# Recurrent mixer, output projection and layer norm of three tiles placed beside the third attention, and modulation chunks spaced out

## The chip, the cores and the metric

The kernel runs on one core of a Trainium2 chip, as one program written engine by engine: TensorE (PE) multiplies, VectorE (DVE), ScalarE (ACT) and GpSimd (POOL) do the elementwise work, SyncE (SP) issues the weight transfers. The metric is the device time of one execution in microseconds. All data are float32. A float32 matmul shows in the trace as two weight loads and two matmul instructions.

## What is computed

Three transformer-like layers over 512 tokens (4 tiles of 128) of width 1024:

```python
# layers 0 and 1: adaptive modulation, two attentions each
mod = silu(c) @ w_ada[layer] + b_ada[layer]          # 1024 x 3072, per layer: shift, scale, gate
h = rmsnorm(x, g_pre) * (1 + scale) + shift
y = even_mixer(h) if layer == 0 else odd_mixer(h)    # (mla + window) or (differential + forgetting)
x = x + gate * rmsnorm(y, g_post)
# layer 2
h = x @ w_in
o_nsa = compressed, selected and window attention, 6 heads
o_sb  = stick_breaking(...)                          # 4 heads
o_hg  = hgrn2_mixer(...)                             # 6 heads, a recurrence over the tokens:
#   b = cumsum(log f);  att[t, s] = sum_d q[t,d] k[s,d] exp(b[t,d] - b[s,d])
#   o = att @ v + (q * exp(b)) @ state;  state = exp(b_last) * state + (k * exp(b_last - b)).T @ v
o_hg = o_hg * rsqrt(mean(o_hg^2) + eps) * hg_norm_w
mixed = concat(o_nsa, o_sb, o_hg) * silu(z)
out = layer_norm(ALPHA * x + mixed @ w_out)
```

## The kernel before

**Attention as a sequence of steps.** `attention(L)` (L = 0, 1, 2) walks over value units, one per head and tile of 128 queries: 64, 48 and 88 of them. In step r TensorE issues the scores of the unit two ahead (`LOOK`, L879), waits for the probabilities of this unit and transposes them (L894), and multiplies the previous unit with its values (L857). DVE masks and takes the row maximum (L1952), ACT takes the exponential (L1320) and copies the transposed block (L1168). Each engine runs its own instructions strictly in the order written, so a wait in one holds everything behind it. Scores and transposes have two buffers each, probabilities four.

**Fill.** Between these, `filler(n)` gives TensorE other matmuls, one contraction step of a 128x512 tile at a time: projections not needed yet, or output projections of finished tiles. `FILLERS[L]` lists weight chunks with their tiles in order, `SPREAD[L]` says (number of tiles, over how many steps), `UNITS` how many fill units a tile has (8 if not listed). `tile_done` on DVE and ACT evicts a tile in the step in which it ends; slower sequences (`chains`) advance by one stage a step.

**Weights.** `ring` has three slots of 2 MB. Chunk n goes to slot n mod 3, and SP waits until the chunk three before it has been used (L709).

**First attention.** Its fill is seven gate tiles (steps 0 to 19), then the eight chunks of `w_ada` for the gate of layer 0 and the modulation of layer 1 (steps 20 to 33): `adas` sums a chunk with 32-column matmuls (L811), `adac` or `adag` (L796, L803) add its strips. Then tiles 0 to 2 of the output projection and the input transposes of layer 1. In front of chunk (0, 5) SP also issues the replication `rel_rows` (L699), in front of (1, 4) two rows (L702, L703).

**Third attention.** Groups: for each query tile the heads of the compressed, selected and window branches, then at the end the stick-breaking heads of all four tiles (steps 72 to 87). Its fill is seven weight chunks, over 82 of the 88 steps. `hf` starts the forget-gate chain `forget_tile`, three times, with a reciprocal on DVE (L1848). POOL forms the recurrence's operands: `differences(c)` (15 instructions), then ACT's `exponentials(c)` (L1351 to L1356), then `operands(c)` (16 instructions), all from L1540; chunks 0 and 1 of these are started in the last steps (`HG_EARLY`).

**Recurrence, after the attention.** For each tile c: level products of three pairs of heads, written into the score and transpose banks (L1087, L1090), their sums on DVE (L1632), `outputs` (L1103, L1108), the state update (L1135), the head norm; beside it the output tile of c-1: transposes `mT` (L910), two `y` halves (L920), layer norm over DVE and ACT, two passes on POOL (L1540) and the store. Tile 3 comes last.

## Time and profile before

| | us |
|---|---|
| median of three runs | 1452.41 |
| lowest, highest | 1451.28, 1458.86 |
| the profiled execution | 1457.49 |
| its span, first to last instruction | 1455.7 |
| TensorE busy | 1280.3 (88%) |
| VectorE busy | 553.7 (38%) |
| ScalarE busy | 427.3 (29%) |
| GpSimd busy | 112.3 (8%) |
| mean granted TensorE clock | 0.911 |

Numbers of TensorE instructions are larger than those of matmuls in the code, since each float32 matmul is two. The granted clock is relative to 2.4 GHz; 0.5 is the lower of the two levels, 1.2 GHz.

### The profile page before, as it was taken

To read this page: it belongs to the slowest core of one execution; us is meant where nothing else is said; L and a number is where in the kernel's file an instruction comes from. 1 tells how busy PE (TensorE), PEld (TensorE's weight loads), DVE (VectorE), ACT (ScalarE), POOL (GpSimd) and SP (SyncE) were. 2 spreads that over 40 slices of the span, in tenths; PEclk is the share of its full clock that TensorE was granted. 3 is DMA by queue.
4 is the path that set the end of the run, shared out by engine and by line. 5 is a ranking of instruction groups with operands and counts; after the bars stand their busy time and mean duration, and the time that the engine had idled before them with its cause. 6 is when DMAs were issued, how large, how long until landed. Compare 5 with 4: busy or idle time off the path is not lost.

```text
span 1455.7 us, 15110 instructions
## 1 busy us (share of the span) xinstructions
PE 1280.3 (88%) x5264; PEld 706.9 (49%) x5264; DVE 553.7 (38%) x1422; ACT 427.3 (29%) x1086; POOL 112.3 (8%) x140
## 2 busy tenths in 40 slices
PE   4989989679998999989999989989998999966974
PEld 1555555335554444334455555555453555545541
DVE  3233223323445420234442433112124731667871
ACT  0133025313433101322224322114233543651211
POOL 0000000000001000000000000000000000384722
PEclk7889999868988999999999999989998999956987
DMA  9221311468000430242111005241101111000000
GB/s 349 80 87 48 126 58 58 159 218 227 1 1 1 116 58 16 61 100 58 58 59 58 1 1 139 59 159 44 44 0 44 44 59 58 1 0 31 1 30 29
DMA packets 60258, 99.71 MB, mean 69 GB/s; under 512 B 12068, under 2 KB 22129, under 8 KB 60184
## 3 DMA queue, kind: packets, MB, share of 16 engines
q1 hardware_dynamic: 54370, 93.58, 20.7%
q10 hardware_dynamic: 5814, 5.18, 1.1%
q8 instruction: 43, 0.70, 0.2%
q14 instruction: 31, 0.25, 0.1%
HBM read 96.60 MB, written 4.08 MB: 69 GB/s over the span
## 4 chain that ended last, share of the span: by engine, by line
PE 72%; DVE 13%; ACT 5%; DMA 4%; issue 3%; POOL 2%; ACTq 1%; SPq 0%; DVEq 0%; POOLq 0%
PE PR L827 29%; PE SC L879 7%; PE OB L857 6%; PE PT L739 6%; PE PR L739 4%; PE OB L739 4%; PE SC L739 4%; DMA ring<-in_w_ada 4%; PE PT L894 3%; PE PR L920 3%; DVE d L1632 2%; DVE stage L1632 2%; POOL arena L1540 2%; PE PR L811 1%; DVE tok L1632 1%
## 5 line engine op out<-in xcount | busy, mean ns | idle before, releaser
L827 PE MATMUL PR<-ring,hT 128*128 128x512 f32 (+1 forms) x784 | 380.2, 599 | 6.9 <-DVE hT L1671 4.1
L1320 ACT ACTIVATE stage<-stage,nmax 128x256 f32<-128x256 f32 (+7 forms) x200 | 103.7, 519 | 350.3 <-DVE nmax L1952 328.1
L827 PEld LDWEIGHTS PR<-ring,hT 128*128 128x128 f32 x784 | 137.0, 198 | 115.9 <-issue 96.4
L857 PEld LDWEIGHTS OB<-arena,pts 128*128 128x128 f32 (+3 forms) x880 | 133.7, 205 | 104.8 <-issue 84.0
L879 PE MATMUL SC<-arena 64*128 64x256 f32 (+15 forms) x432 | 150.5, 459 | 10.0 <-DVE nmax L1952 10.0
L827 PE MATMUL PR<-hT,ring 128*128 128x512 f32 (+1 forms) x304 | 155.1, 634 | 0.0
L1540 POOL TENSOR_TENSOR arena<-arena 128x192 f32<-128x192 f32 (+1 forms) x118 | 80.1, 679 | 830.7 <-PE OB L857 782.8
L857 PE MATMUL OB<-arena,pts 128*128 128x64 f32 (+4 forms) x880 | 134.2, 283 | 9.9 <-ACT pts L1168 9.9
L894 PEld LDWEIGHTS PT<-ident,stage 128*128 128x128 f32 (+3 forms) x440 | 58.4, 147 | 124.3 <-issue 59.0
L894 PE MATMUL PT<-ident,stage 128*128 128x128 f32 (+3 forms) x440 | 87.7, 291 | 29.8 <-ACT stage L1299 12.2
L1168 ACT ACTIVATE pts<-PT 128x256 f32<-128x256 f32 (+7 forms) x200 | 80.7, 404 | 52.7 <-issue 19.7
L1952 DVE CUSTOM_DVE_ANT_0 stage<-SC,causal 128x128 f32<-128x128 f32 (+3 forms) x96 | 47.2, 491 | 115.7 <-issue 52.9
L827 PEld LDWEIGHTS PR<-hT,ring 128*128 128x128 f32 (+1 forms) x304 | 52.3, 194 | 57.2 <-issue 55.9
L879 PEld LDWEIGHTS SC<-arena 64*128 64x128 f32 (+2 forms) x432 | 62.7, 194 | 25.0 <-DVE nmax L1952 10.4
L1952 DVE CUSTOM_DVE_ANT_0 stage<-SC,arena 128x128 f32<-128x128 f32 (+7 forms) x72 | 28.0, 388 | 119.8 <-PE SC L879 59.5
L920 PE MATMUL PR<-ring,hT 128*128 128x512 f32 x128 | 63.3, 649 | 6.1 <-DVE hT L2176 6.1
L739 PE MATMUL PR<-ring,hT 128*128 128x512 f32 (+5 forms) x160 | 51.8, 481 | 3.9 <-ACT hT L1211 2.0
L739 PE MATMUL SC<-ring,hT 128*128 128x512 f32 (+3 forms) x144 | 51.2, 515 | 0.0
L739 PE MATMUL PT<-ring,hT 128*128 128x512 f32 (+4 forms) x144 | 50.0, 502 | 0.0
L920 PEld LDWEIGHTS PR<-ring,hT 128*128 128x128 f32 x128 | 25.8, 209 | 36.1 <-issue 29.5
L1636 DVE TENSOR_SCALAR t<-PR 128x512 f32<-128x512 f32 (+3 forms) x29 | 17.4, 600 | 64.9 <-PE PR L827 53.7
L739 PEld LDWEIGHTS PR<-ring,hT 128*128 128x128 f32 x160 | 28.6, 203 | 24.0 <-issue 17.7
(337 smaller groups left out, 1300.2 us busy)
## 6 DMA issues: line engine op xcount, KB each, us to landing
ring<-in_w_ada SPq DMA_DIRECT2D x12, 2048.0 KB, 18.6
ring<-in_od_w_in SPq DMA_DIRECT2D x8, 2048.0 KB, 14.2
ring<-in_w_in SPq DMA_DIRECT2D x5, 1536.0 KB, 6.7
ring<-in_ev_w_in SPq DMA_DIRECT2D x3, 2048.0 KB, 7.9
ring<-in_w_in SPq DMA_DIRECT2D x3, 2048.0 KB, 9.7
ring<-in_ev_w_out SPq DMA_DIRECT2D x2, 2048.0 KB, 8.0
ring<-in_od_w_out SPq DMA_DIRECT2D x2, 2048.0 KB, 8.6
ring<-in_w_out SPq DMA_DIRECT2D x2, 2048.0 KB, 7.8
```

Source lines behind the costliest of these rows:

```text
L739: mm = pe.matmul(dst, lhs(k), rhs(k), start=(k == 0), stop=(k == K - 1))
L827: mm = pe.matmul(dst, l, r, start=(k == 0), stop=(k == KT - 1))
L857: mm = pe.matmul(ob[:, h * w:h * w + w], pts[0:rows_, v % 2, n * P:n * P + P], vb, start=(n == 0), stop=(n == len(blocks) - 1))
L879: pe.matmul(SC[s % 2][:, 0:n], q, k, start=True, stop=True).then_inc(s_done, 1)
L894: tr = pe.transpose(PT[v % 2][0:w, b * P:b * P + P], pb[:, s % NP, b * P:b * P + w], ident[:, :])
L920: mm = pe.matmul(b[:, :], hT[:, k, i * P:i * P + P], W[:, k, :], start=(k == 0), stop=(k == KT - 1))
L1168: return act.activation(dst, src, ACT.Copy, scale=scale)
L1320: give(act.activation(pb[:, s % NP, 0:n], zm[:, s % 2, 0:n], ACT.Exp, bias=nmax[:, row, c:c + 1], scale=-1.0, accum_out=rsum[:, row, c:c + ...
L1540: return pool.tensor_tensor(dst, a, b, op)
L1632: return dve.tensor_tensor(dst, a, b, op)
L1636: return dve.tensor_scalar(dst, a, s1, None, op0)
L1952: give(dve.tensor_tensor_reduce(out=z, in0=SC[s % 2][:, 0:n], in1=mask, scale=-scale, scalar=start, op0=ALU.add, op1=ALU.min, accum_out=nm ...
```

## The change

Three things, besides what they need in buffers.

1. In the first attention each `w_ada` chunk is followed by a gate tile, over four steps a pair. The two gate chunks keep their ring slots for that long and all eight `w_ada` chunks use the remaining slot (`ring_slots`). A chunk's strip sum comes after the next chunk's matmuls.
2. In the third attention the stick-breaking heads move to steps 18 to 33, behind tile 0 of the other branches. The projections are done by step 37. Steps 38 to 87 are filled with the recurrence of all four tiles and the output projection and layer norm of tiles 0 to 2. The level products become one tile per head (24 instead of 12 pairs), in the two banks of the fill, with their sums on DVE (`level_sums`) per head as well; head norm and layer norm become chains over steps. `exponentials(c)` starts at steps 26, 38, 49 and 60 and takes three steps. POOL makes differences and operands as early as the buffers allow, and its four output tiles last. The ring slot of `nz` and parts of `hT`, `grow`, `window` hold what stood in the score banks and the arena; two ring slots are left for the weights of that phase.
3. Small moves: in attention 1 `next_input(2, 0)` comes before tile 2's output; `finish_gates()` comes first among DVE's evictions of a step.

Behind the attention only tile 3 remains: `mT`, `y`, layer norm, store.

```diff
+def strip_sum(chunk_):
+
+    return ("adag", chunk_[0], chunk_[1] - 4) if chunk_[1] >= 4 else ("adac", *chunk_)
+
+
+STRIP_CHUNKS = [(0, 4), (1, 0), (0, 5), (1, 1), (1, 2), (1, 4), (1, 3), (1, 5)]
+GATES = [("gate0", 1, 0), ("gate0", 0, 1), ("gate0", 1, 1), ("gate0", 0, 2), ("gate0", 1, 2), ("gate0", 0, 3),
+         ("gate0", 1, 3)]
...
 FILLERS = [
-    [(("w", "gate0", 0), [("gate0", 0, i) for i in range(1, T)]),
-     (("w", "gate0", 1), [("gate0", 1, i) for i in range(T)])]
-    + [(("ada", 0, 4), [("adas", 0, 4)]), (("ada", 1, 0), [("adas", 1, 0), ("adag", 0, 0)]),
-       (("ada", 0, 5), [("adas", 0, 5), ("adac", 1, 0)]), (("ada", 1, 1), [("adas", 1, 1), ("adag", 0, 1)]),
-       (("ada", 1, 2), [("adas", 1, 2), ("adac", 1, 1)]), (("ada", 1, 4), [("adas", 1, 4), ("adac", 1, 2)]),
-       (("ada", 1, 3), [("adas", 1, 3), ("adag", 1, 0)]),
-       (("ada", 1, 5), [("adas", 1, 5), ("adac", 1, 3), ("adag", 1, 1)]),
+    [(("w", "gate0", 0), []), (("w", "gate0", 1), [])]
+    + [(("ada", *STRIP_CHUNKS[0]), [("adas", *STRIP_CHUNKS[0])])]
+    + [part for now, then, gate in zip(STRIP_CHUNKS, STRIP_CHUNKS[1:], GATES) for part in
+       ((("w",) + gate[:-1], [gate]), (("ada", *then), [("adas", *then)]), (("w",) + gate[:-1], [strip_sum(now)]))]
+    + [
        (("wo", 0, 0), []),
-       (("wo", 0, 1), finish_tile(0, 0) + finish_tile(0, 1) + next_input(1, 0) + finish_tile(0, 2)
-        + next_input(1, 1))],
...
+     (("wo", 2, 0), []),
+     (("wo", 2, 1), [("kbT", 0)] + grams(0, 0, 6) + [("ho", 0), ("st", 0), ("kbT", 1)] + grams(1, 0, 6)
+      + [("ho", 1), ("st", 1)] + finish_tile(2, 0)[:3] + [("kbT", 2)] + finish_tile(2, 0)[3:] + grams(2, 0, 1)
+      + finish_tile(2, 1)[:3] + grams(2, 1, 2) + finish_tile(2, 1)[3:] + grams(2, 2, 6) + [("ho", 2), ("st", 2)]
+      + grams(3, 0, 4) + finish_tile(2, 2)[:3] + grams(3, 4, 5) + finish_tile(2, 2)[3:] + grams(3, 5, 6)
+      + [("ho", 3)])],
 ]
...
-SPREAD = [[(7, 20), (16, 14), (4, 8), (4, 8), (6, 8), (2, 6)], [(15, 15), (4, 12), (4, 8), (4, 7), (6, 6)], [(21, 68), (4, 14)]]
+SPREAD = [[(4, 5)] + [(3, 4)] * 6 + [(5, 9), (2, 1), (4, 10), (2, 1), (2, 9), (2, 5)], [(15, 15), (4, 12), (4, 8), (2, 1), (2, 5), (2, 1), (2, 1), (2, 5)], [(11, 15), (14, 23), (8, 7), (2, 1), (6, 5), (1, 1), (1, 1), (2, 1), (2, 4), (2, 4), (2, 1),
+           (2, 4), (2, 4), (3, 3), (1, 1), (1, 1), (4, 4), (2, 1), (2, 3), (2, 3), (1, 1)]]
...
-        groups += [("sb", i, [[("sb", h, i)] for h in range(SBH)]) for i in range(T)]
+            if i == 0:
+                groups += [("sb", j, [[("sb", h, j)] for h in range(SBH)]) for j in range(T)]
...
+def ring_slots(chunks):
+
+    slots, turn, kept = {}, 0, {}
+    for c in chunks:
+        if c[0] == "ada" and c[1:] in STRIP_CHUNKS:
+            slots[c] = kept["ada"]
+            continue
+        if c[0] == "wo" and c[1] == 0:
+            slots[c] = kept["gate", c[2]]
+            continue
+        if "nz" in kept and turn % RING == kept["nz"]:
+            turn += 1
+        slots[c] = turn % RING
+        turn += 1
+        if c[:2] == ("w", "gate0"):
+            kept["gate", c[2]] = slots[c]
+            kept["ada"] = turn % RING
+        if c == ("w", "nz"):
+            kept["nz"] = slots[c]
+    return slots
...
-HG_EARLY = (78, 84)
+EXP_STEPS = (26, 38, 49, 60)
...
+            def level_products(c, h):
+                m, r = h // 2, h % 2
+                q = slice(MN * r, MN * r + MN)
+                b = begin(("gram", c, h))
+                for l in range(NLEV):
+                    for j in range(2):
+                        u = slice(HB * j, HB * j + HB)
+                        if l < NLEV - 1:
+                            a = b_ = Y[c % 2][q, l, m, u]
+                        else:
+                            w = slice(c * P + HB * j, c * P + HB * j + HB)
+                            a, b_ = a2["key"][q, m, w], a2["hq"][q, m, w]
+                        pe.matmul(b[u, HB * l:HB * l + HB], a, b_, start=True, stop=True)
+                pe.matmul(b[0:HB, GW:GW + HB], Y[c % 2][q, NLEV - 1, m, 0:HB],
+                          Y[c % 2][q, NLEV - 1, m, HB:P], start=True, stop=True).then_inc(pr_done, 1)
+
+            def outputs(c):
+                freed(pe, ("hi", c))
+                b = begin(("ho", c))
+                if c > 0:
+                    freed(pe, ("st", c - 1))
+                yield
+                pe.wait_ge(gs_s, HGH * (c + 1))
+                for m in range(HP):
+                    if c > 0:
+                        pe.matmul(b[:, m * P:m * P + P], qb[c % 2][:, m, :], state[m], start=True, stop=False)
+                    for r in range(2):
+                        h = 2 * m + r
+                        mm = pe.matmul(b[:, h * MN:h * MN + MN], att[h], a2["hi"][:, c, h * MN:h * MN + MN],
+                                       start=(c == 0), stop=(c == 0 or r == 1))
+                mm.then_inc(pr_done, 1)
...
+            def exponentials(c):
+
+                t = slice(c * P, c * P + P)
+                act.wait_ge(y_s, c + 1)
+                link(act.activation(Y[c % 2][:, 0:4], Y[c % 2][:, 0:4], ACT.Exp))
+                yield
+                link(act.activation(Y[c % 2][:, 4:NLEV], Y[c % 2][:, 4:NLEV], ACT.Exp))
+                yield
+                link(act.activation(kb[c % 2], kb[c % 2], ACT.Exp))
+                link(act.activation(qb[c % 2], a2["b"][:, :, t], ACT.Exp))
+                if c >= 2:
+                    freed(act, ("st", c - 2))
+                give(act.activation(dec[c % 2], a2["b"][:, :, c * P + P - 1:c * P + P], ACT.Exp), ye_s, c + 1)
+                yield
...
-            nsa = [g for g, e in enumerate(plan[2]) if e[0] != "sb"][-1]
             pool.wait_ge(hgf, 3)
-            pool.wait_ge(pv_done, last_v[2, nsa] + 1)
-            pool.wait_ge(masked, s_no["sb", 0, 0])
+            used(pool, ("nz", T - 1))
             differences(0)
-            drained(pool, ("hq", 2))
+            for m in range(3):
+                freed(pool, ("hq", m))
             operands(0)
-            used(pool, ("hi", T - 1))
-            differences(1)
-            operands(1)
-            for c in range(T + 1):
-                if c + 2 < T:
-                    differences(c + 2)
-                if c + 2 < T:
-                    operands(c + 2)
-                if c >= 1:
-                    output_tile(c - 1)
+            sticks = [g for g, e in enumerate(plan[2]) if e[0] == "sb"][-1]
+            pool.wait_ge(pv_done, last_v[2, sticks] + 1)
+            for c in range(1, T):
+                differences(c)
+                operands(c)
+            for i in range(T):
+                output_tile(i)
...
+            def level_sums(c, h):
+                b, w = take(dve, ("gram", c, h)), att[h]
+                link(tt(gm, b[:, 0:GW], levels, ALU.mult))
+                release(dve.tensor_copy(w[0:HB, HB:P], b[0:HB, GW:GW + HB]), ("gram", c, h))
+                link(tt(gm[:, 0:3 * HB], gm[:, 0:3 * HB], gm[:, 3 * HB:6 * HB], ALU.add))
+                link(tt(gm[:, 0:HB], gm[:, 0:HB], gm[:, HB:2 * HB], ALU.add))
+                link(tt(gm[:, 2 * HB:3 * HB], gm[:, 2 * HB:3 * HB], gm[:, 6 * HB:7 * HB], ALU.add))
+                link(tt(w[0:HB, 0:HB], gm[0:HB, 0:HB], gm[0:HB, 2 * HB:3 * HB], ALU.add))
+                give(tt(w[HB:P, HB:P], gm[HB:P, 0:HB], gm[HB:P, 2 * HB:3 * HB], ALU.add), gs_s, HGH * c + h + 1)
...
```

## Rows read from the trace of the kernel before

**Rows 1.** The page, 40 equal slices of the span, busy tenths and clock tenths.
```profile
PE   4989989679998999989999989989998999966974
...
PEclk7889999868988999999999999989998999956987
```
**Rows 2.** By stretch: length, PE, PEld, DVE, ACT, POOL busy, granted clock, DMA.
```profile
275.00:335.00 60.00, 40.65 (x184) 19.33 (x180) 12.80 (x33) 11.14 (x35) 0.00 (x0) 0.66 0.74 266
...
978.00:1090.00 112.00, 108.98 (x378) 57.41 (x378) 27.71 (x121) 40.56 (x133) 0.00 (x0) 0.98 0.09 29
1090.00:1160.00 70.00, 63.67 (x207) 32.77 (x207) 41.28 (x88) 27.98 (x66) 0.00 (x0) 0.89 0.14 46
1160.00:1240.00 80.00, 78.05 (x320) 44.13 (x319) 20.56 (x66) 32.42 (x79) 0.00 (x0) 0.99 0.15 53
1240.00:1315.00 75.00, 59.08 (x227) 38.09 (x226) 48.17 (x78) 44.11 (x86) 45.90 (x62) 0.77 0.00 1
1315.00:1409.00 94.00, 74.06 (x910) 49.37 (x909) 76.66 (x157) 17.50 (x32) 46.02 (x65) 0.80 0.05 18
1409.00:1455.70 46.70, 26.02 (x63) 11.44 (x61) 13.06 (x30) 6.60 (x15) 12.99 (x6) 0.77 0.08 34
```
**Rows 3.** Waits of PE, 195 to 460 us: total, times, longest.
```profile
PE PR L811 <- DMA ring<-in_w_ada: 17.9, 2, 11.1
```
**Rows 4.** In order of time, 1352 to 1362 us: start, length, instructions, count.
```profile
1352.62 7.09 PE L920 MATMUL PR<-ring,hT 128*128 128x512 f32 x16
...
1361.09 1.04 PE L1087 MATMUL SC<-arena 64*64 64x64 f32 x56
```
**Rows 5.** In order of time, 264 to 330 us.
```profile
269.70 0.87 SPq L699 DMA_DIRECT2D rel_rows<-rel_row  x1
270.62 16.84 SPq L709 DMA_DIRECT2D ring<-in_w_ada  x3
...
270.70 1.07 PE L811 MATMUL PR<-ring,cond 128*32 128x512 f32 x8
...
291.11 1.94 PE L811 MATMUL PR<-ring,cond 128*32 128x512 f32 x8 [11.08 <-DMA ring<-in_w_ada]
```
**Rows 6.** The twelve loads of w_ada, from issue to landing.
```profile
DMA to landing us min/median/max: 7.9/18.6/25.2
```
**Rows 7.** The chain of work, 1085 to 1170 us: a unit, and one reciprocal of three.
```profile
1086.59 0.39 PE OB L857 x4
1086.98 0.33 PE SC L879 x2
...
1112.94 3.36 DVE arena L1848
```
**Rows 8.** POOL in order of time, from 1240 us.
```profile
1246.98 10.41 POOL L1540 TENSOR_TENSOR arena<-arena 128x192 f32<-128x192 f32 x15 [782.84 <-PE OB L857]
1269.90 25.98 POOL L1540 TENSOR_TENSOR arena<-arena 128x192 f32<-128x192 f32 x30 [12.50 <-ACT arena L1356]
```
**Rows 9.** The chain of work, 1240 to 1320 us.
```profile
1296.88 2.45 ACT arena L1351
...
1303.57 1.59 DVE d L1930
```
**Rows 10.** In order of time, 1398 to 1456 us.
```profile
1410.05 0.56 DVE L2210 COPY d<-OB 128x384 f32<-128x384 f32 x1
1410.36 2.35 POOL L1540 TENSOR_TENSOR x<-ring,arena 128x1024 f32<-128x1024 f32 x1
1410.64 2.49 DVE L1632 TENSOR_TENSOR d<-d 128x384 f32<-128x384 f32 x1
...
1424.61 17.03 PE L920 MATMUL PR<-ring,hT 128*128 128x512 f32 x32 [6.07 <-DVE hT L2176]
```
**Rows 11.** Groups of DVE instructions, 1315 to 1456 us: count, busy, mean ns.
```profile
L1632 DVE TENSOR_TENSOR ring<-stage 64x128 f32<-64x128 f32 x24 | 10.0, 416 | 0.8
...
L1632 DVE TENSOR_TENSOR stage<-SC,grow 128x896 f32<-128x896 f32 x6 | 6.6, 1092 | 2.4 <-PE SC L1090 2.2
```

More of the change, by code:

```diff
@@ L177, in chunk @@
     def chunk(name, names):
-        chunks.append(name)
+        if name not in chunks:
+            chunks.append(name)
         jobs.extend(names)
@@ L668, in two_block_kernel @@
             chunk_of[name] = ("w",) + name[:-1]
-        chunk_no = {c: n for n, c in enumerate(chunks)}
         w_val, w_view, filled = {}, {}, [0] * RING
@@ L688, in _ @@
             for n, c in enumerate(chunks):
-                if n >= RING:
-                    sp.wait_ge(pr_done, chunk_end[chunks[n - RING]])
+                earlier = [o for o in chunks[:n] if slot[o] == slot[c]]
+                if earlier:
+                    sp.wait_ge(pr_done, chunk_end[earlier[-1]])
                 if c == ("w", "gate0", 0):
@@ L776, in tile_matmuls @@
                 kind = name[0]
+                if kind == "kbT":
+                    pe.wait_ge(yr_s, name[1] + 1)
+                    transposes(name, [kb[name[1] % 2][:, m, :] for m in range(3)])
+                    yield
+                    return
+                if kind == "gram":
+                    pe.wait_ge(yr_s, name[1] + 1)
+                    level_products(*name[1:])
+                    yield
+                    return
+                if kind == "ho":
+                    yield from outputs(name[1])
+                    return
+                if kind == "st":
+                    c = name[1]
+                    freed(pe, ("kbT", c))
+                    b = begin(name)
+                    for m in range(3):
+                        mm = pe.matmul(b[:, m * P:m * P + P], kbT[:, m * P:m * P + P],
+                                       a2["hi"][:, c, m * P:m * P + P], start=True, stop=True)
+                    mm.then_inc(pr_done, 1)
+                    yield
+                    return
                 if kind in ("mT", "hT"):
@@ L1138, in _ @@
-            for _ in output_tile(T - 1):
-                pass
+            for name in finish_tile(2, T - 1):
+                whole_tile(name)
         @block.scalar
@@ L1269, in tile_done @@
                     input_half(*name[1:3])
+                elif kind == "kbT":
+                    c = name[1]
+                    b = take(act, name)
+                    if c:
+                        used(act, ("st", c - 1))
+                    release(copy(kbT, b[:, 0:384]), name)
+                    if c == 0:
+                        act.dma_start(lng, rows(A["ln_g_2"], D)).then_inc(ln_in, 16)
+                        act.dma_start(lnb, rows(A["ln_b_2"], D)).then_inc(ln_in, 16)
+                elif kind == "ho":
+                    chains.append(head_norm())
+                elif kind == "y" and name[1] == 2:
+                    if name[3] == 1:
+                        chains.append(layer_norm(name[2]))
                 elif kind == "y" and name[3] == 0:
@@ L1497, in _ @@
             attention(2)
[L1498 to L1517 removed]
+            for chain in chains:
+                for _ in chain:
+                    pass
+            mixed_half(2, T - 1)
+            for _ in layer_norm(T - 1):
+                pass
         @block.gpsimd
@@ L1825, in tile_done @@
                 elif kind == "hf":
+                    if i == 0:
+                        used(dve, ("nz", T - 1))
+                        for h in range(4, HGH):
+                            link(dve.memset(att[h][HB:P, 0:HB], 0.0))
                     chains.append(forget_tile(i))
```

397 lines of the change are left out of this document (153 added, 244 removed).

## Prediction

> **What bounds the kernel now.** I read the views from coarse to fine: the page's forty slices, busy time by stretch, TensorE's waits, then single pieces in order of time. The slices [rows 1] show TensorE at 8 to 9 tenths nearly everywhere, so the kernel is one long matmul stream, and time can only come from its holes and from stretches at half clock. Two places stand out. One is slices 8 and 9, in the middle of the first attention. The other is the last eight, where TensorE's share falls to 4 to 7 tenths in half of them and the granted clock to 5 to 8.
>
> The stretches [rows 2] size them. From 275 to 335 us TensorE is busy 40.7 of 60 us at a clock of 0.66: 19.3 us idle, and about 40.7 x 0.34 = 13.8 us of the busy time is owed to the clock. The idle time is `w_ada` weights that haven't landed [rows 3]. From 1240 to 1315 us it is busy 59.1 of 75 at 0.77, and from 1315 to 1409, the recurrence behind the attention, 74.1 of 94 at 0.80. In contrast 978 to 1090 and 1160 to 1240 are nearly full at 0.98 and 0.99.
>
> **Full-clock work.** Busy time times clock is what TensorE would need at full clock; the product is my estimate. The third attention (978 to 1315) has 109.0 x 0.98 + 63.7 x 0.89 + 78.1 x 0.99 + 59.1 x 0.77 = 286 us of it in 337 us [rows 2]. The recurrence stretch has 74.1 x 0.80 = 59 us in 94 us; the last `y` half of tile 2, some 7 us (seven or eight matmuls of 0.9 us, [rows 4]), lies just behind it, so what moves into the attention is 66 us.
>
> **Part 1: modulation chunks.** Now eight `w_ada` chunks run back to back, each 2 MB load covered by 2 to 4 us of matmuls. The change puts one gate tile (8 steps of the contraction, so 16 instructions; such 16 take 7.1 us in [rows 4], 6.9 when nothing cuts in) between each pair, over four attention steps. Nothing is added or removed on an engine; the order changes, and the ring: the gates keep two slots, so all eight chunks pass through one slot, and a load can start only when the chunk before it has been used. The period is 6.9 (gate) + 2 x 1.06 (chunk, [rows 5]) + 1.0 (its sum) + four attention units = 12.4 us (values and scores of a unit of two key blocks take 0.39 + 0.33 us, [rows 7]; I take 0.6 for a whole unit of one block), of which some 10 us lie between the end of one chunk's matmuls and the start of the next. The shortest landing of such a load is 7.9 us [rows 6], so six of the seven loads should hide. The one for (0, 5) doesn't: in front of it in SP's queue stands the copy `rel_rows` of 1920 KB, and before it landed 20.5 us after its issue (270.6 to 291.1, [rows 5]). About 10 us of stall is left there less one step of slack, so 8. The two rows in front of (1, 4) are short; 0 to 1 us. Gain 33 - 8 = 25 us, bounds 10 and 33. The output tiles of this attention now begin five steps earlier and spread over 35 steps instead of 30; I cost that at nothing, since TensorE is 9 tenths busy there with either spacing. The same for the reordering at the end of attention 1.
>
> **Part 2: the recurrence as fill.** Work of 66 us goes beside the attention, whose spread now covers all 88 steps where 82 had fill. Removed: the 94 us stretch; what stands there now is the attention itself, longer. The terms:
> - 286 + 66 = 352 us at full clock.
> - The level products are now issued per head (24 tiles) where pairs of heads alternated between upper and lower partitions. 56 of a pair's 60 instructions take 1.04 us [rows 4], so a pair about 1.1 to 1.3. No row shows one head alone. Bounds: no change, or twice as long per instruction, 12 x 1.3 = 16 us. I take 8, as the two column halves still alternate.
> - Ordinary losses of a filled attention: 978 to 1090 and 1160 to 1240 take 192 us for 184 us of full-clock work, 4.3%, so 15 us.
> - The forget-gate chain (`hf`, three reciprocals of 3.36 us each on VectorE, [rows 7]) now costs 70 - 56.7 = 13.3 us in 1090 to 1160, 11 above the ordinary. It runs in fewer steps now but the steps are longer (about 4.9 us of fill each). The same 11 us.
> - New waits, 0 to 25 us, taken at 10. The stick-breaking units, whose scan alone takes VectorE 1.59 us at the largest size [rows 9], come beside the `hf` chain. ScalarE waits in order for POOL's differences at steps 26, 38, 49 and 60; queued behind that wait are the exponentials and copies that TensorE needs two steps later. POOL needs 10.4 us for the differences, 26 for operands plus the next differences while VectorE is busy [rows 8]; steps 38 to 49 are 11 steps of 3.3 us, so it keeps up, with little to spare at step 45, where TensorE waits for `kbT` 1.
> So the attention should last 352 + 8 + 15 + 11 + 10 = 396 us.
>
> What goes: the end of the old attention, where ScalarE sat behind POOL's differences(1) and the last stick-breaking unit behind ScalarE [rows 9], 16 us idle and 13.6 of clock in 1240 to 1315, and the 35 us of idle and clock in the recurrence. What is late next is the final tile, which nothing covers: `ho` 3, its norm, transposes, 17.0 us of `y` at lowered clock, a layer norm across ScalarE and VectorE, two POOL passes of 2.35 us [rows 10]. Before it takes 46.7 us (1409 to 1455.7). VectorE still drains tile 2's layer norm ahead of its half of the transposes, so nothing is saved; one more attention group must be finished first, 2.5 us. So 49 us.
>
> The sum: 396 + 49 = 445 us against 477.7 (978 to 1455.7), a gain of 32; with part 1, 57. The profiled execution is 1457.5 us, its span 1455.7; the median of the three runs is 1452.4. 1457.5 - 57 = 1400.5 and 1452.4 - 57 = 1395.4: I predict **1398 us**.
>
> **The rivals.**
> - *The fill is free.* The POOL hand-overs and the load of (0, 5) hide in the slack of two steps, and level products cost what they did: 8 + 10 + 8 us less, 1372. For it: attention at 978 to 1090 loses only 3 us. Against: every chain before it that hung on VectorE did cost.
> - *Level products double.* The full 16 us, 1406. TensorE: Matmul & The Clock Gate of the Trainium skill (Part 3, what overlaps) says that a weight load overlaps running matmuls only when their row groups differ; a head's fifteen products stay in one row group. By that rule the term is 16, not 8. The trace shows only the alternating order, at 1.04 / 56 = 19 ns an instruction, which fits the rule without testing it.
> - *VectorE becomes the bound.* A head's seven operations come to about 2.3 us ([rows 11], 1.09 for 896 columns, so 0.6 for 448; 0.42 for a small one while POOL works), plus 0.5 for the unit and 0.5 for its share of group finishing: 3.3 us against 2.6 to 3.1 of TensorE. And POOL's 100 us now run beside the softmax: in [rows 10] a 128x384 product takes VectorE 2.49 us while a POOL pass runs, and the copy of as many elements just before it 0.56. One us on each of 24 products is 24 us, 1422. By GPSIMD Engine Reference of the Trainium skill (Specifications), POOL shares its SBUF interfaces with VectorE, and operations with two SBUF inputs contend. This row agrees.
> - *Part 1 brings nothing* (loads hide no better than now): 1423.
> - *The single slot starves TensorE*: this one ends slower than before. If a chunk lands as the median of the twelve loads does, 18.6 us [rows 6], against 10 us of cover, seven loads stall 8.6 us each, 60 us in all, 52 more than forecast. After each stall the matmuls run at half clock (1.94 instead of 1.07 us for the same eight, [rows 5]), some 4 us each by estimate, 28. 1398 + 80 = 1478. It decides from a landing of about 10 + (57 + 8) / 7 = 19 us without the clock, 15 with it. Against it: the long landings belong to loads queued behind others, and in the changed kernel each is alone.
>
> **Chances.** Forecast 0.50; free fill 0.14; doubled products 0.10; VectorE 0.15; nothing from part 1 0.05; starving 0.06. The bounds of the terms (part 1 from 10 to 33, products 0 to 16, waits 0 to 25) put the forecast's own range at 1375 to 1430; with the second to fifth case most of the way, 1366 to 1438. A measurement of this kernel can tell about 0.5%, 7 us, from no change: faster is below 1445, slower above 1460. All but the starving case lie below 1445; for mixtures of the bad ends I move a little: faster 0.88, same 0.05, slower 0.07.
>
> **What would show it.** Part 1: no wait on `w_ada` over 1 us but one of about 8 near the first third of the first attention, and the clock at 1.0 around it. Part 2: the last attention about 396 us long at 0.95 to 0.98 with no slice under 8 tenths, then 49 us. Level products: 30 instructions a head in 0.6 us (no change) or 1.2. VectorE: its share in the steps with products above 9 tenths, and TensorE's waits naming VectorE's masks. The forecast is wrong if TensorE waits for POOL at `kbT` or the products, or if ScalarE waits long for the differences; then the hand-over steps are too early.

## The result, and the profile after

| | before | after |
|---|---|---|
| median, us (4 runs each) | 1453.0 | **1491.6** (1487.6 to 1492.5) |
| ratio to before, 95% interval | | 1.026 [1.022, 1.029] |
| span of the profiled execution, us | 1455.7 | 1490.4 |
| mean granted TensorE clock | 0.911 | 0.897 |

The forecast was 1398 us; the change makes the kernel 2.6% slower. The slices of the page show where, against [rows 1]:

```profile
PE   4989987899898899899989989899969998896974
PEclk7889997999998999999999999999989956895686
```

The last quarter of the row of clocks has two hollows, of 5 and 6 and of 5 and 6 again, in slices where TensorE's share is 9, 8, 6 and 9 tenths. By stretch (length, then busy time of PE, PEld, DVE, ACT and POOL, granted clock, DMA share, GB/s), to be read beside [rows 2]; the third attention now runs from 966 to 1441 us:

```profile
966.00:1080.00 114.00, 109.18 (x316) 54.50 (x316) 23.80 (x93) 33.02 (x98) 0.00 (x0) 0.97 0.09 28
1080.00:1125.00 45.00, 33.53 (x85) 15.36 (x84) 39.23 (x61) 21.01 (x45) 7.39 (x13) 0.89 0.11 35
1125.00:1190.00 65.00, 64.90 (x262) 40.01 (x261) 35.02 (x60) 34.97 (x71) 24.98 (x34) 1.00 0.17 57
1190.00:1280.00 90.00, 75.69 (x553) 56.51 (x551) 58.62 (x175) 27.62 (x74) 39.87 (x62) 0.60 0.10 36
1280.00:1340.00 60.00, 56.85 (x293) 32.15 (x294) 19.51 (x65) 24.19 (x58) 15.28 (x18) 0.97 0.03 10
1340.00:1405.00 65.00, 51.87 (x339) 36.38 (x334) 38.59 (x114) 13.20 (x36) 4.71 (x2) 0.54 0.02 9
1405.00:1441.00 36.00, 35.02 (x209) 22.01 (x209) 11.22 (x31) 11.26 (x23) 0.00 (x0) 0.98 0.01 1
1441.00:1490.40 49.40, 20.80 (x61) 10.66 (x60) 15.92 (x33) 5.45 (x13) 9.36 (x4) 0.67 0.05 21
```

The stretches at 0.60 and 0.54 are those in which products (`gram`) stand beside the attention. In between, `y` projections do, at 0.97.

For the rest I split every 5 us window in three: idle time of TensorE, clock loss (busy time x (1 - clock)) and work (busy time x clock, what it would take at full clock). Summed from the last `nz` projections, just ahead of the third attention, to the end of the span. Each row is one profiled execution; executions of one kernel differ by some us (after 1487.6 to 1492.5, even_few_both 1448.1 to 1467.2), so differences of a few us between rows say little:

| kernel | from | length | idle | clock loss | work | ratio to before |
|---|---|---|---|---|---|---|
| before | 968 | 487.7 | 69 | 40 | 379 | 1 |
| after | 958 | 532.4 | 77 | **70** | 386 | 1.026 |
| few_products | 958 | 521.7 | 83 | 69 | 369 | 1.021 |
| few_sums | 958 | 522.7 | 66 | 75 | 383 | 1.018 |
| few_both | 958 | 510.3 | 71 | 68 | 372 | 1.007 |
| few_both_wide3 | 958 | 541.8 | 72 | **29** | 441 | 1.031 |
| even_mix | 958 | 521.8 | 73 | 63 | 387 | 1.021 |
| even_few_both | 958 | 504.6 | 63 | 69 | 373 | 1.003 |
| paired | 958 | 536.1 | 97 | 66 | 373 | 1.027 |
| mix_hz | 958 | 529.8 | 77 | 71 | 382 | 1.029 |
| wide_beside_products | 958 | 565.8 | 75 | 85 | 406 | 1.050 |
| wide6 | 958 | 629.4 | 74 | 43 | 513 | 1.092 |

The 44.7 us that this part grew by are 8 of idle time, **30 of clock** and 7 of work; 10 come back because it starts 10 us earlier. The change filled the recurrence's idle time as it meant to, and idle time as a whole didn't fall.

### The profile page after: what moved, and what is told of

It reads as the page before. It is cut to its first block, busy times and chain, and to the rows that moved or that the text cites. A ratio compares the mean times of both kernels' runs of the same rounds, so it can differ in the third digit from the quotient of the medians.

```text
span 1490.4 us, 15244 instructions
## 1 busy us (share of the span) xinstructions
PE 1307.6 (88%) x5264; PEld 736.4 (49%) x5264; DVE 567.0 (38%) x1513; ACT 428.0 (29%) x1090; POOL 108.9 (7%) x140
## 4 chain that ended last, share of the span: by engine, by line
PE 74%; DVE 14%; ACT 4%; issue 3%; DMA 3%; ACTq 1%; POOL 0%; DVEq 0%; SPq 0%; POOLq 0%
PE PR L929 32%; PE SC L981 7%; PE OB L959 6%; PE PT L775 5%; PE PR L775 4%; PE OB L775 4%; PE SC L775 4%; PE PT L996 3%; DVE d L1654 3%; DMA ring<-in_w_ada 3%; PE PR L815 2%; DVE tok L1654 1%; PE OB L929 1%; PE PR L790 1%; DVE arena L1953 1%
## 5 line engine op out<-in xcount | busy, mean ns | idle before, releaser
L929 PE MATMUL PR<-ring,hT 128*128 128x512 f32 (+1 forms) x896 | 429.2, 599 | 14.3 <-DVE arena L1877 6.3
L959 PEld LDWEIGHTS OB<-arena,pts 128*128 128x128 f32 (+2 forms) x880 | 136.3, 209 | 86.7 <-issue 70.5
L981 PE MATMUL SC<-arena 64*128 64x256 f32 (+15 forms) x432 | 157.4, 476 | 11.5 <-DVE nmax L2057 11.5
L929 PE MATMUL PR<-hT,ring 128*128 128x512 f32 (+1 forms) x304 | 145.8, 620 | 4.4 <-ACT arena L1176 4.4
L959 PE MATMUL OB<-arena,pts 128*128 128x64 f32 (+3 forms) x880 | 138.3, 288 | 7.7 <-ACT pts L1176 7.6
L996 PE MATMUL PT<-ident,stage 128*128 128x128 f32 (+2 forms) x440 | 90.8, 298 | 38.1 <-DVE stage L1654 19.8
L996 PEld LDWEIGHTS PT<-ident,stage 128*128 128x128 f32 (+2 forms) x440 | 58.2, 148 | 132.2 <-issue 77.0
L1176 ACT ACTIVATE pts<-PT 128x256 f32<-128x256 f32 (+7 forms) x200 | 80.7, 404 | 87.1 <-issue 44.7
L1567 POOL TENSOR_TENSOR ring<-arena 128x192 f32<-128x192 f32 (+1 forms) x30 | 17.5, 585 | 670.2 <-DVE arena L1965 658.6
L1567 POOL TENSOR_TENSOR arena<-arena 128x192 f32<-128x192 f32 (+1 forms) x62 | 38.2, 616 | 62.3 <-ACT arena L1263 44.6
L1196 ACT ACTIVATE t<-t 128x512 f32<-128x512 f32 (+3 forms) x32 | 16.8, 525 | 87.4 <-DVE t L1658 87.4
```

Source lines behind the costliest of these rows:

```text
L929: mm = pe.matmul(dst, l, r, start=(k == 0), stop=(k == KT - 1))
L959: mm = pe.matmul(ob[:, h * w:h * w + w], pts[0:rows_, v % 2, n * P:n * P + P], vb, start=(n == 0), stop=(n == len(blocks) - 1))
L981: pe.matmul(SC[s % 2][:, 0:n], q, k, start=True, stop=True).then_inc(s_done, 1)
L996: tr = pe.transpose(PT[v % 2][0:w, b * P:b * P + P], pb[:, s % NP, b * P:b * P + w], ident[:, :])
L1176: return act.activation(dst, src, ACT.Copy, scale=scale)
L1567: return pool.tensor_tensor(dst, a, b, op)
```

## Experiments

**Which part loses?** part1_alone is the kernel before with the modulation chunks spaced as in the kernel after, and nothing else:

```diff
...
+    + [part for now, then, gate in zip(STRIP_CHUNKS, STRIP_CHUNKS[1:], GATES) for part in
+       ((("w",) + gate[:-1], [gate]), (("ada", *then), [("adas", *then)]), (("w",) + gate[:-1], [strip_sum(now)]))]
...
```

> The kernel before with only the spaced modulation chunks (and the earlier finish_gates). The changed kernel starts its second layer's projections 6 us earlier than the one before, where 25 were forecast. If the two parts add up, this kernel gains about 6 us: ratio to before 0.996, and all of the 38 us of loss is the third attention's. If the parts interact it comes out otherwise, 0.98 to 1.00.

Measured 1447.7 us, ratio 0.995 [0.992, 0.998]. So the first part gains some 6 us, and the rest of the change, which is the third attention but for the small moves in attention 1, loses all of it and 38 more.

**Is it the want of wide matmuls?** One 128x512 matmul of no use ahead of each head's products:

```diff
                 b = begin(("gram", c, h))
+                pe.matmul(b[:, :], ident[:, :], hi[:, 0:512], start=True, stop=True)
```

> The changed kernel with one more full-size matmul (128x512, float32, its result overwritten at once) in front of each of the 24 product tiles: 24 x 0.86 = 21 us of added work at full clock, twice that at half. Theory A, the stream of small matmuls leaves TensorE at half clock and TensorE is then the bound (31 us lost to the clock in 1190 to 1280, 25 in 1340 to 1405): the clock in those stretches rises, the added work is paid back, and the time stays at 1475 to 1500. Theory B, VectorE's sums are the bound there and the low clock is only its symptom: TensorE has slack, the clock may rise, the time stays within 5 us of 1491. Theory C, TensorE is the bound and the clock does not depend on what it runs: 1491 + 42 = 1533.

Measured 1526.7 us, 35 more than after, nearest to theory C. The clock stays at half (0.54 in 1200:1240), and the clock loss grows from 70 to 85.

mix_hz puts three of the four `hz` projections between the products of chunks 0 and 1:

> The changed kernel with three of the four hz projection tiles (24 contraction steps of 128x384) taken out of steps 26 to 37 and put between the product tiles of chunks 0 and 1, so that no step there has products alone; nothing is added. Theory A: the clock holds in the first product stretch, some 20 to 30 of its 31 us come back, 1465 to 1475. Theory B: VectorE stays the bound there and the moved work hides behind it, so the steps it left get shorter by 15 us: 1475 to 1480 with or without a better clock. Theory C: no change, 1491.

```diff
-     (("w", "hz"), [("hz", i) for i in range(T)]),
+     (("w", "hz"), [("hz", 0), ("kbT", 0)] + grams(0, 0, 2) + [("hz", 1)] + grams(0, 2, 3) + [("hz", 2)]
+      + grams(0, 3, 6) + [("ho", 0), ("st", 0), ("kbT", 1)] + grams(1, 0, 4) + [("hz", 3)]),
...
```

Measured 1494.5 us, ratio 1.029 [1.025, 1.033]: no change, theory C.

wide6 gives six such matmuls a head:

> Six 128x512 matmuls of no use ahead of each of the 24 heads' products. Their 144 matmuls cost 31 us at full clock and 61 us at half. Theory 'the clock comes back once wide matmuls hold most of the time': the lost 56 us of these stretches come back in large part, and the time is 1491 + 31 - 40 or so = 1470 to 1500. Theory 'the clock does not come back in these stretches': 1545 to 1555. In between, the clock returns for a part.

Measured 1589.9 us, outside both expectations, since I had sized such a matmul too low. From the table one costs (513 - 386) / 144 = 0.88 us of work, and 144 of them 127 us. The time rose by only 98, because 27 us of clock loss are gone. The same 40 us of wide6, by stretch (TensorE is full, the clock 1.00):

```profile
1200.00:1240.00 40.00, 40.00 (x277) 21.53 (x276) 17.30 (x50) 5.19 (x15) 10.61 (x16) 1.00 0.01 1
```

So the clock does come back beside products, where the run with one such matmul a head had not brought it back.

**Are the products the cause, or VectorE's sums?** few_products leaves out levels 1 to 5 of the products, few_sums cuts the sums from seven VectorE instructions to three, few_both does both:

```diff
-                for l in range(NLEV):
+                for l in (0, NLEV - 1):
...
-                link(tt(gm, b[:, 0:GW], levels, ALU.mult))
-                release(dve.tensor_copy(w[0:HB, HB:P], b[0:HB, GW:GW + HB]), ("gram", c, h))
...
+                link(dve.tensor_copy(w[0:HB, HB:P], b[0:HB, GW:GW + HB]))
+                release(tt(w[0:HB, 0:HB], b[0:HB, 0:HB], levels[0:HB, 0:HB], ALU.mult), ("gram", c, h))
+                give(tt(w[HB:P, HB:P], levels[HB:P, 0:HB], levels[HB:P, HB:2 * HB], ALU.add), gs_s, HGH * c + h + 1)
```

> The changed kernel without the products of levels 1 to 5 (10 of 15 matmuls of each head left out; the sums are still formed, so the output differs). At half clock a head's 30 instructions take 1.97 us in the trace, so this takes 24 x 1.3 = 31 us off TensorE at half clock, 16 at full. If TensorE at half clock is the bound in the product steps (A, C): 10 to 30 us faster, 1460 to 1480. If VectorE's sums are (B): within 5 us of 1491.

> The kernel after, with VectorE's sums of each head's levels cut from seven instructions to three (the sums of the middle levels are left out, so the output is not the reference's); all products stay. VectorE loses 24 heads x about 2.0 us (one 128x448 of 0.63, one 128x192 of 0.39, two 128x64 of 0.31, two 64x64 of 0.32) = some 45 us. Theory 'VectorE makes TensorE wait and so takes its clock down': the product stretches get their clock back and the time falls by 25 us or more, below 1467. Theory 'TensorE itself, at the low clock, is the bound' : within 8 us of the kernel after, 1483 to 1492.

> Both cuts together: levels 1 to 5 of the products and the sums of those levels are left out (the output is not the reference's). What is left of a head is 5 products and 3 VectorE instructions. If the stream of products and sums is the whole cause, the third attention returns to about 400 us and the time to 1430 or below. If each of the two alone was hidden by the other, few_sums and few_products each give under 10 us but this one 40 or more. If it stays above 1470, the cause is neither: then it is something else about these steps, such as where the other work stands.

Measured 1482.4, 1481.9 and 1466.0 us: 9, 10 and 26 us less than after, each outside the ranges named beforehand (for few_products 1460 to 1480, for few_sums below 1467 or 1483 to 1492, for few_both 1430 or below, or above 1470). Neither is the bound alone: when the products are thin, TensorE waits for the sums (idle 83), and when the sums are thin, TensorE at half clock has no less to do (clock loss 75). With both cut the kernel is still slower than before (1.007 [1.005, 1.009]), and its clock loss has hardly moved. In few_both 1200:1240 TensorE is full, at half clock; few_both_wide3 is the same kernel with three wide matmuls a head:

> few_both (levels 1 to 5 of the products and VectorE's sums of them left out, so the output is not the reference's) with three 128x512 matmuls of no use ahead of each head. By wide6 and the kernel after such a matmul costs (295 - 207) / 144 = 0.62 us of TensorE at full clock: 72 of them 44 us, or 89 at half. Theory 'the clock is low for want of wide matmuls, not for VectorE': the clock is back to full through most of 1195:1280, and the time is 1466 + 44 - 30 = 1480 or a little more. Theory 'only the wait on VectorE or on the softmax sets the clock': 1510 to 1555.

few_both, 1200 to 1240 us, by stretch:

```profile
1200.00:1240.00 40.00, 39.79 (x199) 28.21 (x199) 19.72 (x72) 15.42 (x41) 19.34 (x31) 0.50 0.14 52
```

few_both_wide3, the same:

```profile
1200.00:1240.00 40.00, 38.76 (x197) 21.34 (x197) 14.65 (x50) 12.56 (x32) 19.23 (x31) 0.96 0.14 54
```

The clock is 0.50 in the one and 0.96 in the other, with the same idle time in the table. Measured 1497.9 us. At the 0.88 us found above, 72 such matmuls are 63 us at full clock and 127 at half; 1466 + 63 - 39 us of clock loss won back = 1490, against 1593 with the clock still at half. By this run's own row such a matmul costs (441 - 372) / 72 = 0.96 us of work, which gives 1496. The clock answers as the first theory says. Its time, 1480 or a little more, was too low, since it took 0.62 us a matmul. With it comes the size of the trap: the wide work costs more than the clock that it gives back.

**Does it matter where the wide work stands?** even_mix deals the kernel's own wide work out: `hz` beside chunk 0, `y` of tile 0 beside chunk 1, and so on. even_few_both is the same with thin products and sums.

```diff
...
-     (("wo", 2, 1), [("kbT", 0)] + grams(0, 0, 6) + [("ho", 0), ("st", 0), ("kbT", 1)] + grams(1, 0, 6)
+     (("wo", 2, 1), grams(0, 5, 6) + [("ho", 0), ("st", 0), ("kbT", 1)] + grams(1, 0, 3) + finish_tile(2, 0)[:2]
+      + grams(1, 3, 4) + [("y", 2, 0, 0)] + grams(1, 4, 6) + [("y", 2, 0, 1)]
...
```

> The kernel after with the wide work (the hz projections, the mixed tiles 0 to 2) dealt out evenly between the 24 heads of products, instead of in blocks of their own: hz beside chunk 0, output tile 0 beside chunk 1, tile 1 beside chunk 2, tile 2 beside chunk 3. Nothing is added or left out. Theory 'stretches in which TensorE has narrow matmuls alone lose the clock, and VectorE is full at the same time': each 5 us has some wide work and under 3 us of VectorE, the clock loss of the third attention falls from 65 us to 30 or less, and the time to 1440 to 1465. Theory 'where the wide work stands doesn't matter': 1487 to 1497, as mix_hz.

> even_mix (wide work dealt out between the heads) with few_both's cut (levels 1 to 5 of the products and VectorE's sums of them left out, so the output is not the reference's). even_mix still lost 62 us of clock from 958 us on, few_both 67. Theory 'the clock needs both, few short stalls and wide work in every step; the stream of products and sums gives the stalls': with the stream thin and the wide work even, the clock loss falls to 45 us or less and the time to 1440 to 1455. Theory 'thin or not, the attention steps themselves lose the clock when no projections of the size before.py gave them (2.4 units a step over all 82 steps) stand beside them': the loss stays at 55 to 65 us and the time at 1458 to 1466.

even_mix measured 1482.3 us, 9 less than after and in neither theory's range, with 63 us of clock loss where I expected 30 or less. even_few_both measured 1461.3 us, 1.003 [1.000, 1.006], clock loss 69: the second theory's time, and rather more than its loss of 55 to 65. Even here 30 us together have no projection in them (the groups of these 30 us hold 12.4 us of scores, 9.1 of values, 7.7 of transposes and only 4.5 of products), and TensorE is full at half clock in them; windows of 10 us of even_few_both:

```profile
1350.00:1360.00 10.00, 10.00 (x43) 5.86 (x42) 7.67 (x28) 3.65 (x10) 0.00 (x0) 0.50 0.00 0
1360.00:1370.00 10.00, 10.00 (x43) 5.96 (x42) 5.63 (x14) 2.19 (x5) 4.71 (x2) 0.50 0.00 0
1370.00:1380.00 10.00, 10.00 (x34) 7.01 (x32) 2.05 (x6) 2.64 (x6) 0.00 (x0) 0.50 0.14 54
```

The kernel before has the clock at 1.00 through 1200:1240, beside the same kind of attention steps. There the groups of PE (count, busy, mean ns) are:

```profile
L827 PE MATMUL PR<-hT,ring 128*128 128x512 f32 x32 | 16.5, 612 | 0.0
L827 PE MATMUL PR<-ring,hT 128*128 128x384 f32 x12 | 5.2, 512 | 0.0
```

That is 21.7 of 40 us of projections. The kernel after has 6.1 us of 128x512 in the 90 us from 1190 to 1280. So the clock is lost not to the products alone: with products and sums thin (few_both) the loss is 68 of 70 us. In the 30 us above the attention's own steps run at half clock with 4.5 us of products beside them and no projection.

**Do the products cost double?** paired gives the products of two heads alternately to both row halves, into two banks:

```diff
-                        pe.matmul(b[u, HB * l:HB * l + HB], a, b_, start=True, stop=True)
+                        for r in range(2):
+                            q = slice(MN * r, MN * r + MN)
+                            pe.matmul(bs[r][u, HB * l:HB * l + HB], a, b_, start=True, stop=True)
```

> The kernel after, with the products of two heads given alternately to the upper and the lower row half, into two banks, as before.py gives them, and in the order of jobs that this needs. Theory 'the products cost double because they are given for one row half at a time': 348 products in 1190:1280 took 22.7 us of TensorE; half of that goes, and as much in the second stretch, so 15 to 25 us less, 1467 to 1476. Theory 'the low clock alone': the clock stays at half and less product work gives under 8 us, since the stretches wait on VectorE next.

PE in order of time, at full clock (start, length, count), 30 products of one head in the kernel after:

```profile
1435.68 1.03 PE L815 MATMUL PR<-arena 64*64 64x64 f32 x28
1436.55 0.28 PE L816 MATMUL PR<-arena 64*64 64x64 f32 x2
```

and 60 of a pair in paired:

```profile
1434.81 1.04 PE L818 MATMUL PR<-arena 64*64 64x64 f32 x56 [0.51 <-DVE tok L1667]
1435.64 0.31 PE L821 MATMUL PR<-arena 64*64 64x64 f32 x4
```

Twice the products in the same 1.14 us (1434.81 to 1435.95; 1.15 for the 30). Work falls by 13 us, as 12 x 1.14 says, and the time doesn't: 1495.3 us, ratio 1.027 [1.023, 1.031]. The idle time rises from 77 to 97, since a pair needs two banks that VectorE must have drained (from 1190 to 1440 us four waits on its copy, 19.5 us in all, the longest 8.8).

**The tail.** tail_wait holds GpSimd's passes of output tile 2 until VectorE has normed the last heads:

```diff
+                if i == T - 2:
+                    pool.wait_ge(hof, T)
```

> The kernel after, with GpSimd's two layer norm passes of output tile 2 held until VectorE has normed the last chunk's heads. Theory 'two VectorE steps of 128x6 in the last chain took 2.27 and 2.18 us, against 0.17 for their like, because GpSimd ran beside them': these two steps take 0.2 us again, the last tile starts 4 us earlier, and the time is 4 us lower, 1485 to 1489. Theory 'they were late for another reason': no change, and the two steps stay at 2 us.

In the kernel after, in order of time:

```profile
1450.39 0.17 DVE L1654 TENSOR_TENSOR rt<-rr 128x6 f32<-128x6 f32 x1
1450.50 2.34 POOL L1567 TENSOR_TENSOR tok<-tok,hT 128x1024 f32<-128x1024 f32 x1 [63.23 <-DVE tok L1659]
1450.59 2.27 DVE L1654 TENSOR_TENSOR rt<-rt,rv 128x6 f32<-128x6 f32 x1
1452.91 2.35 POOL L1567 TENSOR_TENSOR x<-tok,hT 128x1024 f32<-128x1024 f32 x1
1453.10 2.18 DVE L1654 TENSOR_TENSOR rr<-rr,rt 128x6 f32<-128x6 f32 x1
```

and in tail_wait:

```profile
1447.70 0.17 DVE L1656 TENSOR_TENSOR rt<-rt,rv 128x6 f32<-128x6 f32 x1
1448.11 0.17 DVE L1656 TENSOR_TENSOR rr<-rr,rt 128x6 f32<-128x6 f32 x1
```

The two steps are back at 0.17 us, and the median is 1486.3, 5 less, as expected: some 4 of them are these two steps. All four runs (1485.3 to 1486.9) lie below the lowest of after.

**The first part, and a version that beats both.** regate moves a gate projection ahead of the first modulation chunk; lastln gives the last output tile's two layer norm passes to VectorE; best is both.

```diff
-SPREAD = [[(4, 5)] + [(3, 4)] * 6 + [(5, 9), (2, 1), (4, 10), (2, 1), (2, 9), (2, 5)],
+SPREAD = [[(2, 2)] + [(3, 4)] * 6 + [(2, 4), (5, 8), (2, 1), (4, 10), (2, 1), (2, 9), (2, 5)],
...
+                if i == T - 1:
+                    link(ts(yb, yb, lam[:, 7:8], ALU.add, rr[:, 0:1], ALU.mult))
+                    dve.wait_ge(ln_in, 32)
+                    dve.wait_ge(x_s, 3 * T - 1)
+                    link(tt(yb, yb, lng, ALU.mult))
+                    give(tt(x[:, i, :], yb, lnb, ALU.add), x_s, 3 * T)
+                    return
```

> part1_alone (only the first part of the change, on before.py) with one gate projection moved ahead of the first modulation chunk of the first attention, and the last chunk given four steps of its own. The chunk (0, 4) was waited for 9.0 us in part1_alone, with the clock at half for some 10 us behind it. Theory 'the load had no cover': that wait goes, 9 us of idle and 4 of clock, of which some come back as shorter steps later: 1434 to 1442 against 1447.7. Theory 'waits move, as with the change itself, which took 33 us of losses out of 275:335 and gave 26 back': within 4 us of part1_alone.

> part1_alone with the two layer norm passes of the last output tile on VectorE instead of GpSimd. They took GpSimd 2.34 us each and nothing ran beside them; VectorE's 128x896 pass is 1.09 us, so 128x1024 about 1.24. The end comes 2.2 us earlier: 1445.5 against 1447.7. Read it from the trace, since 0.15% can hardly be told by the times.

> regate and lastln together: the sum of the two, 1432 to 1440, and so faster than before.py by 1% and than after.py by 3.5%, if the waits do not move; 1443 to 1446 if they do.

regate measured 1450.0 us (0.997 [0.995, 1.000]), not distinguishable from part1_alone: its expectation had put the long wait down to chunk (0, 4), while it belongs to (0, 5), which regate left as it was. lastln measured 1444.2 (0.993 [0.991, 0.995]), by its times not distinguishable from part1_alone either; the trace shows the gain. Its last two passes, on VectorE in place of 2.34 us each on GpSimd:

```profile
1436.98 1.23 DVE L1662 TENSOR_TENSOR ring<-ring,arena 128x1024 f32<-128x1024 f32 x1
1438.24 1.23 DVE L1662 TENSOR_TENSOR x<-ring,arena 128x1024 f32<-128x1024 f32 x1
```

best measured 1447.6 (0.995 [0.993, 0.997]), above both ranges named for it and no better than lastln; it carries regate's order, but no run shows that this is the reason. rel_later goes for the wait on (0, 5):

```diff
-                if c == ("ada", 0, 5):
+                if c == ("wo", 0, 1):
                     sp.wait_ge(rel_out, 16)
```

> part1_alone with the copy of rel_rows (1920 KB) moved in SP's queue from ahead of modulation chunk (0, 5) to ahead of the second output weight chunk of the first attention. The wait of 9.1 us on w_ada in the kernel after belongs to (0, 5), whose load was issued 0.9 us behind that copy and landed 20.0 us later; regate left it in place and so left a wait of 9.4 us. Theory 'the copy ahead makes the load late': the wait goes, with 3 to 5 us of half clock behind it, and 6 to 12 us of time: 1436 to 1442 against 1447.7 of part1_alone. Theory 'any gain in the first attention is eaten by VectorE's later chains': within 3 us of part1_alone.

> rel_later and lastln together: 2.2 us less than rel_later, 1434 to 1440 by the first theory, 1442 to 1446 by the second.

PE's waits from 195 to 480 us (total, times, longest) in rel_later:

```profile
PE PR L857 <- DVE arena L1818: 6.5, 3, 2.3
PE PR L857 <- DMA ring<-in_ev_w_out: 3.9, 1, 3.9
PE SC L909 <- DVE nmax L1982: 3.6, 1, 3.6
```

The wait on `w_ada` is gone, and one of 3.9 us on the output weights, whose load is now the late one, has come. Measured 1444.2 us (0.993 [0.991, 0.996]), between the ranges of its two theories; against part1_alone (0.995) that is not settled either way. With lastln it is **1440.0 us, 0.990 [0.988, 0.993]**, as the first theory had it, though its interval overlaps that of lastln alone: 1.0% faster than before and 3.5% faster than after, with the recurrence left behind the attention.

## Why the prediction was wrong

It missed by 94 us: some 79 in the third attention and behind it (524.4 us from 966, where I had 445 from 978; its first scores start at 966 and, before, at 976), some 15 in the first part (10 gained at the start of the third attention, where I had 25). The range given, 1375 to 1430, is a little narrower than the bounds of its terms added up, 1372 to 1436; neither holds 1492.

- **Full-clock work, 352 + 8 us: right.** The seven stretches from 966 to 1441 hold 362 us of it. The step that was doubted, level products, came out near its upper bound: 12 x 1.14 = 14 us (bounds 0 to 16, taken at 8), by the alternation that paired shows. So the doubled products, a rival worth 8 us, were right in kind, and the sign named for them (30 instructions a head in 1.2 us) is there. The Trainium skill's rule on row groups (TensorE: Matmul & The Clock Gate, Part 3) is borne out by those rows. Halving their time again in paired didn't shorten the kernel.
- **Ordinary losses, 4.3%: this step failed.** I read the rate of loss in 978:1090 and 1160:1240, filled with projections, and applied it to steps filled with products, whose own rate stood in the same [rows 2]: at 1315 to 1409, 94 us for 59 of work. In the product stretches of after (1190:1280 and 1340:1405) 155 us pass for 71.5 of work: 27 idle, 56 clock. Of the forecast's 36 us for all losses (15 + 11 + 10) the attention took 113: 48 idle, 65 clock. I had costed the 35 us of loss in the old recurrence as gone when the work was moved; 83 us of loss stand in the stretches that it moved to. It isn't the stream's alone: few_both thins it and still loses 68 us of clock from 958 on, against 70, so a good part comes from attention steps whose projections were taken away and put ahead of them. No run shares the 83 us out between the two.
- **The forget-gate chain, 11 us: about right.** 1080 to 1125 took 45 us for 30 of work, 14 above the ordinary, with three reciprocals of 3.35 us on VectorE in it. TensorE's three waits there, 11.5 us, name ScalarE.
- **What starts it and what keeps it.** PE in order of time (the last column: idle time before, and its releaser):

```profile
1189.68 1.13 PE L929 MATMUL PR<-ring,hT 128*128 128x384 f32 x3
1192.63 0.28 PE L996 MATMUL PT<-ident,stage 128*15 128x128 f32 x1 [0.83 <-DVE stage L1654]
...
1195.07 0.38 PE L996 MATMUL PT<-ident,stage 128*15 128x128 f32 x1 [0.83 <-DVE stage L1654]
1195.37 1.55 PE L815 MATMUL PR<-ring 64*64 64x64 f32 x24
```

  The last projection ends at 1190.8, short stalls on VectorE's masks follow, and the clock falls at about 1195. It then stays down though TensorE has no idle time (after, windows of 5 us):

```profile
1200.00:1205.00 5.00, 5.00 (x64) 4.11 (x60) 2.39 (x7) 2.23 (x6) 2.02 (x3) 0.50 0.12 45
1205.00:1210.00 5.00, 5.00 (x43) 3.67 (x41) 4.69 (x10) 0.98 (x3) 4.41 (x7) 0.50 0.02 5
1210.00:1215.00 5.00, 5.00 (x40) 3.68 (x40) 4.69 (x10) 0.00 (x0) 4.43 (x6) 0.50 0.00 0
```

  It comes back where projections stand (1280:1340 at 0.97) or are put (wide6, few_both_wide3), so that wide matmuls give it back is shown. That their want alone keeps it down is not. At 1229 us of after, and at 1407, it came back with no projection in front of it. Before 1229 stood 7 us of values, transposes and state products, all 128 rows high and 64 or 128 columns wide, and scores, without a level product; the same two scores of 64x256 then take 0.70 us instead of 1.22:

```profile
1224.93 1.22 PE L981 MATMUL SC<-arena 64*128 64x256 f32 x2
1226.08 1.65 PE L871 MATMUL PR<-arena,ring 128*128 128x128 f32 x6
1227.52 0.63 PE L996 MATMUL PT<-ident,stage 128*128 128x128 f32 x2
...
1229.40 0.70 PE L981 MATMUL SC<-arena 64*128 64x256 f32 x2
```

  Ten us later it fell again, in the second of two waits of 1.7 and 1.8 us. That short stalls start the fall is read from the rows only. What mixture of the kernel's own work would hold the clock stays open: even_mix and even_few_both did not.
- **The price of new waits, 10 us (0 to 25): right in kind, too small.** Idle time in the product stretches is 27 us, 20 of it in ten waits for VectorE's masks (8.4 us in 1190:1280, 11.5 in 1340:1405).
- **VectorE as the bound (1422): half right.** TensorE's waits do name VectorE's masks, as its sign said, but VectorE is busy 58.6 of 90 us and 38.6 of 65, not 9 tenths. Thinning the sums is worth 10 us beside full products and 16 beside thin ones (few_sums against after, few_both against few_products). The contention of POOL and VectorE that it named is shown by tail_wait in the tail, 5 us; what it costs beside the sums no run shows. By GPSIMD Engine Reference of the Trainium skill (Specifications) the two share SBUF interfaces; the rows above, 2.27 us against 0.17, agree.
- **The last tile, 49 us: right** (49.4), with those 5 us of contention in it that I hadn't listed.
- **Part 1, 25 us (10 to 33): at its lower bound or below.** The third attention starts 10 us earlier in after, but 7 in part1_alone (968.8 against 976.3), whose median is 6 lower. One stall of about 8 us at (0, 5) was forecast and is there. PE's waits in after, 195 to 345 us, beside [rows 3]:

```profile
PE PR L912 <- DMA ring<-in_w_ada: 9.1, 1, 9.1
PE PR L929 <- DVE arena L1877: 6.3, 3, 2.4
...
PE PR L904 <- DVE tok L1654: 2.2, 3, 1.0
PE PR L897 <- DVE tok L1654: 1.5, 3, 0.7
```

  and the queue's order behind it:

```profile
219.39 0.89 SPq L735 DMA_DIRECT2D rel_rows<-rel_row  x1
220.32 43.19 SPq L745 DMA_DIRECT2D ring<-in_w_ada  x3
240.34 1.93 PE L912 MATMUL PR<-ring,cond 128*32 128x512 f32 x8 [9.09 <-DMA ring<-in_w_ada]
```

  What I costed at nothing are the other three lines, 10 us: gates and strip sums, dealt out singly, each wait for VectorE to finish with the tile before, where the kernel before waited 1.5 us. With the clock, 195 to 335 us lose 34 us in after and 39 in before, where I had taken 25 off.
- **The single slot starving TensorE**: didn't happen. The median landing of a `w_ada` load is 8.9 us in after, where [rows 6] had 18.6, as most are now alone in the queue.
- **The rival on the slower side** was the wrong one. The one that came, losses that move with the work, had no place in the list, and 0.07 for slower was far too little.

## What to carry to other kernels

A stream that loses time to stalls and to the clock where it stands alone did not shed these losses when it was laid beside other work, and attention steps from which it drove the projections out ran at half clock. Cost the filled stretch with the rate of loss of the poorer of the two, and ask what wide matmuls are left beside it. Before work is moved into a full stretch, sum idle time, clock loss and work apart for both: here the work was forecast within 2 us and the other two were off by 77.

## What the runs showed of the hardware

- TensorE stayed at 1.2 GHz for 20 us and more while it was busy 5.00 of 5 us with 64x64 products, 64-row scores, 128x64 values and 128x128 transposes. Narrow matmuls alone do not settle it: at 1229 us of after the clock came back behind 128x64 and 128x128 matmuls. TensorE: Matmul & The Clock Gate of the Trainium skill (Part 1) ties the clock to how busy the engine has been of late. The rows of 1200 to 1215 us don't agree if busy means the busy time of a profile, in which the ends of matmuls are modelled.
- 60 products of 64x64 that alternate between the row halves take as long as 30 that stay in one: 1.14 and 1.15 us at full clock, 1.97 us each at half.
- A VectorE product of two 128x6 tiles takes 0.17 us, and 2.27 beside one GpSimd pass over 128x1024 of 2.34 us: it lasts for nearly the whole pass.
